# One fused transformer kernel: two ScalarE sine instructions moved ahead of four PSUM evictions, and six VectorE products moved ahead of a layer's input

## The reference

```
ada = silu(c) @ ada_w + ada_b                  # six vectors of 1024
h = rms_norm(x, mix_pre_g) * (1 + sc_m) + sh_m
u_s, q, k, v, g_s, g_a = split(h @ w_in)       # 512, 512, 512, 512, 1024, 1024 wide
lam_bar = exp(lam * dt)
b_bar = ((lam_bar - 1) / lam) * b              # the factor f = (lam_bar - 1) / lam
states = scan(lam_bar, b_bar @ u_s)            # complex, along the 256 tokens
y = real(c_mat @ states) + d_skip * u_s        # then gelu and a gate
q, k = rope(q, positions), rope(k, positions)  # cos and sin of positions * inv_freq
y_a = softmax(q k^T / 8, causal) v
x = x + gt_m * rms_norm((sigmoid(g_s) * (y @ w_s) + sigmoid(g_a) * (y_a @ w_a)) @ w_out)
```

## Time and profile before

| | |
|---|---|
| median of 3 executions | 2579.59 us (2574.77 to 2580.23) |
| the profiled execution, its own time | 2574.77 us |
| span of its profile | 2572.8 us |
| granted TensorE clock, mean | 0.976 of full |
| busy share: TensorE, VectorE, ScalarE, GpSimd | 94%, 42%, 26%, 2% |
| memory traffic | 676.41 MB, mean 263 GB/s |

### The profile page before, as it was taken

One profiled execution on the slowest core, in us unless ns is written; L12 is line 12 of the kernel. 1 busy time (PEld: TensorE's weight loads), 2 busy tenths in 40 slices (PEclk: granted clock), 3 DMA queues, 4 the chain that ended last, 5 costly groups with the idle time before them and its releaser, 6 DMA issues.

```text
span 2572.8 us, 38064 instructions
## 1 busy us (share of the span) xinstructions
PE 2430.2 (94%) x15566; PEld 1772.3 (69%) x15566; DVE 1079.0 (42%) x1567; ACT 673.6 (26%) x829; POOL 42.2 (2%) x34
## 2 busy tenths in 40 slices
PE   7999899999999999999989899779999799998998
PEld 5667644444444444444449899779988799998998
DVE  7773311111111111111137565666564455575653
ACT  2121300000000000000034443444343443434442
POOL 0000000000000000000000000000000000000000
PEclk9999899999999999999999999989999899999999
DMA  8464389999999999999964355335443144543451
GB/s 355 146 233 183 141 356 421 422 422 422 422 422 422 422 422 422 422 422 422 422 291 164 142 185 187 132 111 180 181 147 146 66 173 185 182 148 131 181 182 78
DMA packets 93763, 676.41 MB, mean 263 GB/s; under 512 B 10452, under 2 KB 11096, under 8 KB 11640
## 3 DMA queue, kind: packets, MB, share of 16 engines
q1 hardware_dynamic: 92592, 673.36, 65.8%
q10 hardware_dynamic: 1096, 1.97, 0.2%
HBM read 674.23 MB, written 1.06 MB: 262 GB/s over the span
## 4 chain that ended last, share of the span: by engine, by line
PE 77%; DMA 13%; DVE 6%; ACT 2%; issue 1%; SPq 0%; POOL 0%; DVEq 0%; ACTq 0%; POOLq 0%
PE psum L765 13%; PE psum L457 13%; PE psum L458 13%; PE psum L459 13%; DMA ring<-in_w_exp 13%; PE psum L790 6%; PE psum L749 3%; PE psum L532 2%; PE psum L633 2%; PE psum L471 2%; DVE arena L1442 2%; PE psum L800 1%; DVE arena L1436 1%; PE psum L671 1%; DVE arena_parts L1442 1%; DVE x L1436 1%
## 5 line engine op out<-in xcount | busy, mean ns | idle before, releaser
L458 PE MATMUL psum<-arena_parts,ring_parts 128*128 128x256 f32 x2832 | 809.3, 286 | 0.0
L457 PE MATMUL psum<-h_parts,ring_parts 128*128 128x256 f32 x1920 | 555.2, 289 | 39.2 <-DVE arena_parts L1442 37.9
L458 PEld LDWEIGHTS psum<-arena_parts,ring_parts 128*128 128x128 f32 x2832 | 552.5, 195 | 0.2
L368 DVE TENSOR_TENSOR ring_parts<-ring,ring_parts 128x2048 fp32r<-128x2048 f32 x181 | 414.5, 2291 | 324.6 <-ACT ring_parts L1237 320.1
L459 PE MATMUL psum<-h_parts,ring_parts 128*128 128x256 f32 x1920 | 548.0, 285 | 0.0
L765 PE MATMUL psum<-ring,arena 128*64 128x512 f32 x2176 | 487.0, 598 | 5.1 <-DMA ring<-in_w_exp 5.1
L457 PEld LDWEIGHTS psum<-h_parts,ring_parts 128*128 128x128 f32 x1920 | 373.6, 195 | 49.5 <-issue 32.1
L459 PEld LDWEIGHTS psum<-h_parts,ring_parts 128*128 128x128 f32 x1920 | 373.6, 195 | 0.0
L1237 ACT ACTIVATE ring_parts<-ring 128x2048 fp32r<-128x2048 f32 x181 | 342.3, 1904 | 71.2 <-DMA ring<-in_w_mix 46.5
L765 PEld LDWEIGHTS psum<-ring,arena 128*64 128x64 f32 x2176 | 152.2, 137 | 296.8 <-issue 296.8
L1439 DVE TENSOR_SCALAR arena<-psum 128x512 f32<-128x512 f32 x68 | 47.0, 692 | 616.7 <-ACT arena L1216 459.2
(11 more groups left out here) (250 smaller groups left out, 1875.0 us busy)
## 6 DMA issues: line engine op xcount, KB each, us to landing
ring<-in_w_exp SPq DMA_DIRECT2D x408, 1024.0 KB, 18.8
ring<-in_w_ffn SPq DMA_DIRECT2D x132, 1024.0 KB, 4.8
ring<-in_w_mix SPq DMA_DIRECT2D x49, 1024.0 KB, 4.8
ring<-in_w_ada SPq DMA_DIRECT2D x24, 1024.0 KB, 6.3
ring<-in_w_in SPq DMA_DIRECT2D x16, 1024.0 KB, 11.0
ring<-in_w_out SPq DMA_DIRECT2D x4, 1024.0 KB, 4.8
ring<-in_w_attn SPq DMA_DIRECT2D x2, 1024.0 KB, 4.7
ring<-in_w_ssm SPq DMA_DIRECT2D x2, 1024.0 KB, 8.1
```

The source lines that it names most:

```text
L368: return engine.tensor_tensor(ring_parts[:, s, :], ring[:, s, :], ring_parts[:, RAW + s, :], ALU.subtract)
L457: mm(out, w[0], a[0], start=start, stop=False, **more)
L458: mm(out, w[0], a[1], start=False, stop=False, **more)
```

## The change

On ScalarE the wait for `rope_angles` and the two sines move from behind the fifth eviction (the first half of `k_a`) to behind the second (the second half of `u_s`), and so ahead of both evictions of `q_a` and both of `k_a`. On VectorE the six products that scale `c_re` and `c_im` move from behind `to_h` to ahead of the wait for `ada_summed`. No instruction is added, removed or altered, and SP's, TensorE's and GpSimd's programs stay as they are.

```
                 for i in range(2):
                     pair_out(dst[:, 2 * i:2 * i + 2, :], n)
                     n += 1
-                    if dst is k_a and i == 0:
-                        act.wait_ge(sem("rope_angles"), 1)
-                        go(sin_t, rope_t, ACT.Sin)
-                        go(cos_t, rope_k, ACT.Sin).then_inc(sem("rope_table"), 1)
+                if dst is u_s:
+                    act.wait_ge(sem("rope_angles"), 1)
+                    go(sin_t, rope_t, ACT.Sin)
+                    go(cos_t, rope_k, ACT.Sin).then_inc(sem("rope_table"), 1)
...
             for m in (1, 2, 4, 8, 16, 32):
                 phases(m, view(0, ST, T // 8), view(1024, ST, T // 8))
 
+            c_re, c_im = pa("c_re", ST, 32), pa("c_im", ST, 32)
+            ca, cb, cc, cd = (view(n * 512, ST, 32) for n in range(4))
+            tt(ca, c_re, across(f_re, 32), ALU.mult)
+            tt(cb, c_im, across(f_im, 32), ALU.mult)
+            tt(cc, c_re, across(f_im, 32), ALU.mult)
+            step(tt(cd, c_im, across(f_re, 32), ALU.mult))
+            tt(c_re, ca, cb, ALU.subtract)
+            step(stt(c_im, cc, -1.0, cd, ALU.mult, ALU.subtract))
+
+
             ada_cols = ada[:].rearrange("p a c -> p (a c)")
 
             ada_b, first = pa("ada_b"), 4 * ADA_FIRST
...
             dve.wait_ge(sem("x_in"), 16)
             to_h(coef[:, 0, :], sem("h_scaled"))
-
-            c_re, c_im = pa("c_re", ST, 32), pa("c_im", ST, 32)
-            ca, cb, cc, cd = (view(n * 512, ST, 32) for n in range(4))
-            tt(ca, c_re, across(f_re, 32), ALU.mult)
-            tt(cb, c_im, across(f_im, 32), ALU.mult)
-            tt(cc, c_re, across(f_im, 32), ALU.mult)
-            step(tt(cd, c_im, across(f_re, 32), ALU.mult))
-            tt(c_re, ca, cb, ALU.subtract)
-            step(stt(c_im, cc, -1.0, cd, ALU.mult, ALU.subtract))
```

## The result

The changed kernel took 2592.6 us (median of 5, 2591.2 to 2593.1). The kernel before took 2579.59 us (median of 5, 2574.77 to 2580.23). The medians differ by 13.0 us. The ratio found from all executions is 1.0055, with a 95% interval of 1.0043 to 1.0068: about 14 us slower. The forecast was 2596.6 us, 17.0 us slower, in a range of 2588 to 2603.

A forecast was written before the change was run, and what follows sets the result against it. TensorE was taken to bound the kernel, with 77% of the chain that ended last. A 14.9 us stall plus 2.1 us of clock gave 17.0 us, on the median 2579.6 us: 2596.6 us, range 2588 to 2603.

The forecast's parts named there:

- The wait behind the second eviction: ScalarE stands at `rope_angles` until 81.5 us, so TensorE's fifth pair starts at 82.94 instead of 68.03 us: 14.9 us.
- the rule of eviction n - 2: On TensorE, pair n waits for ScalarE's eviction n - 2; the forecast had the fifth pair wait for the third eviction.
- The products hidden in it: Products of c delay TensorE's early pairs by about 3.9 us, contained in the 14.9 us shift, so costing nothing extra.
- Rival 2: Sines' table load on ScalarE comes after the wait: 1.28 us more, + 18.3 us, 2597.9 us; chance 0.04.
- Rival 3: Both delays add: products of c also move VectorE's angles by 3.86 us, + 20.9 us, 2600.5 us; chance 0.04.
- The clock: TensorE's clock falls to 1.2 GHz around the new 11 us gap: 2.1 us more, bounds nothing and 4 us.
- Nothing swallows it: Rotations, softmaxes and the experts' transfers all follow TensorE, so the whole 17 us reaches the end.
- Rival 4: The experts' transfer stream runs ahead on its own and swallows the delay: 2579.6 us, not slower; chance 0.04.
- Rival 5: Angles ready before 71.9 us, so the wait is short and 3.9 us of TensorE delay remains: 2583.5 us; chance 0.02.
- carrying the sum to the median: Adds the profiled execution's 17.0 us to the earlier kernel's median of 2579.6 us, giving 2596.6 us.
- Rival 1: The stall before the fifth pair without net clock cost: + 14.9 us, 2594.5 us; chance 0.13.

The follow-up runs named there:

- Experiment 1: Kernel before with only the sines and their wait moved behind the second eviction, products of c left behind `to_h`: 2593.04 us against 2577.36, ratio 1.0058.
- experiment 5: Changed kernel with VectorE's sine arguments also moved up to right behind `to_h`: 2578.59 us against 2577.11 for the kernel before, ratio 1.0005.
- experiment 6: Kernel before with only the sines and their wait moved up two evictions, behind the third: 2582.66 us against 2577.11, ratio 1.0022.
- experiment 7: Kernel before with only the sines and their wait moved up one eviction, behind the fourth: 2577.25 us against 2577.11, ratio 1.0002.
- Experiment 3: Changed kernel with 24 added matmuls, results never read, between the fourth and fifth pair: 2589.25 us, ratio to the kernel before 1.0039.
- experiment 4: Kernel before, unchanged, profiled again: median 2578.12 us of eleven executions, ratio 1.0002.
- experiment 9: Kernel before with twelve added matmuls, results never read, in TensorE's waits for conditioning pieces and ahead of the first pair: 2573.05 us, ratio 0.9990.
- experiment 10: Changed kernel with twelve added matmuls, results never read, in TensorE's front waits: 2591.67 us, ratio to the kernel before 1.0054.
- experiment 8: Kernel before with TensorE's third and fourth `rotate` moved into the first half of the product for `v`: 2574.14 us against 2577.11, ratio 0.9994.
- experiment 2: Kernel before with only the six products of c moved ahead of the wait for `ada_summed`: 2579.35 us against 2577.36, ratio 1.0005.

## Why the prediction was right, and where it was off

**The wait behind the second eviction: right.** The angles were ready at 81.6 us whatever the order of ScalarE; two pairs ran; the fifth started at 82.89, forecast 82.94, which is 14.9 us later than before. Experiment 1 shows that this part alone gives the loss, experiment 5 that the loss goes when the angles are early, experiments 6 and 7 that it follows the rule of eviction n - 2.

**The products hidden in it: right for the two profiled executions.** The third pair came at 58.16, 4.2 us later than before (forecast 3.9), and `modulate_re(0)` at 65.33 against 65.26. Rivals 2 and 3, the table behind the wait and the delays added, did not occur: load at 56.95, fifth pair as forecast.

**The clock: right in kind, too small.** The term was 2.1 us and measured 2.9 (9.87 against 6.97 us for the fifth pair). The prediction took the spell behind a 5.8 us gap; the spell behind 10.65 us lasted from the pair's start to about 88 us, over 5 us where 3 to 4 were forecast. Experiment 3 shows by removal that it is the clock. That both gaps in the prediction's trace were followed by slow matmuls was no rule: after the same 2.11 us gap the clock stayed up in experiments 4, 5, 6, 9 and 10.

**Nothing swallows it: right.** 17.75 us at the gates, 17.9 at the experts' stream, 18.1 at the end. The sum of 17.0 against the execution's own time was 1.1 us short. Rivals 4 and 5 are out.

**The step that failed: carrying the sum to the median.** The forecast added 17.0 us to the median as if every execution of before were the profiled one, and took from that one that "no idle time of VectorE lies there that a moved instruction could fill". In the profiled one the last conditioning matmuls ran at full clock and the third pair started at 54.0. In the traces of experiments 1, 6, 7 and 8 the clock had fallen at the conditioning's last matmuls, VectorE waited up to 1.9 us for `ada_summed`, and the third pair started at 56.0 to 56.3 us. The kernel before pays for such a late front, whether the time goes into that wait or into slow first pairs (in experiment 8 the wait is 0.5 us and the first two pairs take 17.07 us). The changed kernel does not: its stall ends with the angles, and these stay at 81.6 because the products of c fill VectorE's wait; without them, in experiment 1, the sines came at 83.14:

```profile
83.14 0.42 ACT L1108 ACTIVATE arena<-arena 128x256 f32<-128x256 f32 x1 [27.06 <-DVE arena L1439]
```

Against experiment 7, which stands for the kernel before with a late front, the gates' first product of the changed kernel comes 122.01 - 106.31 = 15.7 us later instead of 17.75. The products alone (experiment 2, whose trace has the late front too, with columns that end at 36.90) come 108.67 - 106.31 = 2.4 us later, near the 2.0 of the medians.

These 15.7 us are the size of the distance of the medians, 15.4 us. It is an argument from single traces, not a proof: the kernel before itself was profiled twice, each time with its third pair at 54.0 or 54.6 us. The test with the front kept busy points the same way, but its distance of 18.6 us by medians is 16.7 by means. Of the 4.0 us by which the forecast was too high, 2.4 are the median that it started from and 1.6 the change, 17.0 forecast against 15.4. These 1.6 us are small partly by luck: the sum was 1.1 us short of the profiled executions' 18.1, and the medians lay 2.7 us closer together than those.

**What stays open.** How much of the 4.0 us of experiment 9 is the front and how much is a clock fall spared at the gates (its gates ran at full clock, as in experiment 4) was not separated. Nor is the spread of the kernel before accounted for: a late front (2.1 us) and a fall at the gates (1.7 us) make under 4 of its nearly 11 us, no execution near 2580 us was profiled, and with the front kept busy the spread is still 6 us. The nine executions of the changed kernel lie between 2590.0 and 2594.3 us. Rival 1 (14.9 us, no cost of the clock) has the time nearest to the measured one, 2594.5 us, but not the mechanism: the clock did cost 2.9 us.

## What to carry to other kernels

A wait moved up in an in-order engine costs nothing until an instruction queued behind it is needed; find the first engine that needs one, and compare its time with the release, eviction by eviction. A margin of half a microsecond between two engines, read in one execution, is no margin where TensorE's clock can fall ahead of it: read the same place in several executions, and carry a sum to a median only when the profiled execution stands near it. In short waits of TensorE on the critical path, matmuls whose results nobody reads can be worth more than they cost: here 4.0 us by the medians and 2.6 by the ratio, whose interval (0.9981 to 0.9999) ends just short of no gain.

## What the runs showed of the hardware

After the same 2.11 us gap the same 32 matmuls took 8.76 us in one execution of the kernel before and 7.07 us in another. After 10.65 us of idle time the fifth pair took 9.87 us, after 6.72 us the sixth took 9.46, against 7.1 at full clock, and full clock again (7.07) when TensorE was kept working in the gap. In these runs a longer gap cost little more: the same 32 matmuls took 9.46 us after 6.72, 9.87 after 10.65, 10.05 after 10.68 and 9.84 after 14.32 us of idle time (experiment 6, the changed kernel, experiments 10 and 1). The spread of the kernel before, 2572 to 2583 us, goes along loosely with a mean granted clock of 0.977 to 0.971; at 0.975 alone its executions took 2574.7 to 2580.1 us.
